# Two hand-overs between phases reshaped, and the second mixer's sigmoids and products in another order

## The chip, the core and the metric

One core of one Trainium2 chip. The metric is device time in microseconds of one execution; the kernel before has a median of 3087.38 us over three runs (3086.38 to 3090.63).

## The reference

One step of a small two-layer decoder for a prompt of 1024 tokens and a sample group of 8 sequences with 4 new tokens each, all in float32:

```python
h = x
for l in range(2):
    if l == 0:   # mLSTM matrix memory, 8 heads, chunks of 128 tokens; q,k,v,o and gate rows from one w_in
        mix = mlstm_layer(rmsnorm(h, norm_mix[0]), state_c, state_n, state_m, w_in_a, b_i, b_f, head_norm, w_out_a)
    else:        # one shared K/V from h, 16 heads of 64; the sample group also reads 1024 paged past keys
        k, v = split(rmsnorm(h, norm_kv) @ w_kv)
        q = rmsnorm(h, norm_mix[1]) @ w_q_b
        z = q @ k.T / 8 + sb_bias
        A[t, s] = sigmoid(z[t, s]) * prod(sigmoid(-z[t, j]) for s < j < t)      # stick-breaking, s < t
        mix = (A @ v) @ w_out_b
    h = h + mix
    h = h + square(relu(rmsnorm(h, norm_mlp[l]) @ w_up[l])) @ w_down[l]
y = rmsnorm(h, norm_final)
```

Outputs are y, the shared K/V rows and the mLSTM states, for the prompt and for the sample.

## The kernel before

**Data.** The 1024 + 32 tokens (T = 1056) lie along the free axis in NT = 3 tiles of TW = 352; the 1024 features are KT = 8 blocks of 128 partitions. The residual stream is `h`, 128 x 8 x 1056. A dense product of full precision is made from halves: ACT writes the rounded `xhi`, DVE writes `xlo` = x - xhi, GpSimd (POOL) does the same with every weight panel (128 output features, 512 KB; `split_panel`: an optional gain, a cast, a subtraction), and PE issues three matmuls per block. So a full tile of a panel is 24 matmuls of 352 columns (`dense_tile`), and one panel is three tiles. Raw panels and their halves have two buffers each; a panel may be loaded when the one two before it is split.

**Phases.** Each phase is a block in which every engine has its own written-out queue, with a barrier behind it: `constants` (masks, identity, gains), `embed` (x is turned by 36 groups of transposes into `h`), `mixer_a`, `out_and_mlp`, then semaphores are cleared, `mixer_b`, `out_and_mlp`, `final`. A phase's first two weight panels are loaded and split in the phase before (`head_loads`, `head_splits`). A norm is worked in the phase that needs it: `norm_act` gives the high halves of all blocks and their squares, `norm_dve` the low halves and the sum of the squares, `norm_pe` sums it over partitions, `norm_act_rs` makes the inverse root. PE meanwhile has `dense_first`, the first panel's three tiles together, block by block. In `mixer_a` the first panel (`last128`) holds the gate rows; they are stored to `graw` and regrouped by three products with `pick` (L830), which POOL's fills (L686 and on) must precede; the gate chain on DVE and the dense panels, in thirds of a tile (`third`), follow. `h` is put aside in memory (`spill`) so that its space can be used.

**The MLP.** `out_and_mlp` goes through the 4096 inner features in CH = 8 turns of a loop: per turn, four panels of w_up and four of w_down (two halves each); DVE adds each product tile to `h` at L2009, block by block, and PE uses banks 0, 1 and 2.

**The second mixer.** `mixer_b` works 8 pairs of heads, each in 8 slots. A slot is a tile of 128 queries of the prompt, from the longest (slot 0: 1024 keys, two chunks of 512 columns) to the shortest (slots 4 to 7 have one chunk of up to 512). PE computes the scores z into banks 3 and 4, one for each head of the pair (L1455). For each, ACT applies two sigmoids, of z and of -z (L1642, L1643); DVE multiplies up the second along the keys in a scan (L1785) and multiplies the two (L1791). PE turns the weights of the tile before (L1505, "pack" turns), ACT copies what is turned out of the banks (L1696), PE multiplies it with v (L1551). Between them lie turns of the sample's pages, and the next pair's q, k, v panels in thirds of tiles (`THIRDS_AT`); in the last pair there are none. The sample's weights for half of the sequences (`g`) are made at slots 0 and 4: ACT's sigmoids behind the last page turn of the slot before, DVE's scan and product over 1056 columns (`chain_sample`, L1797 and L1800), and PE's turn of them in the same slot ("sat", L1512), all by tables of slots:

```python
QUERIES_AT, SUMS_AT, SAT_AT, VALUES_AT, YS_AT = {-3: 0}, {0: 0, 4: 1}, {0: 0, 4: 1}, {1: 0, 5: 1}, {2: 0, 6: 1}
```

PE takes the turns of a slot in the order of `turns_of`: rows, pages mixed with packs, the sample's weights, its outputs. PE runs its queue in order, as each engine does.

## Time and profile before

| what | value |
| --- | --- |
| median of the runs | 3087.38 us (3086.38 to 3090.63) |
| profiled execution: time, span | 3094.23 us, 3092.4 us |
| mean granted TensorE clock | 0.974 |
| PE busy | 94% |
| DVE busy | 45% |
| ACT busy | 26% |
| POOL busy | 24% |

The profiled execution is one more execution of the same program, 0.2% above the median; rows are of it. In a timeline a row is start, duration, engine, line of kernel.py, operation, output and inputs, shapes, how many alike in a row (xN), and in brackets how long the engine had stood before it and what ended that. "PEq" or "SPq" is an engine's sequencer, "bank" an accumulation bank of PE.

### The profile page before, as it was taken

To read this page: it belongs to the slowest core of one execution; us is meant where nothing else is said; L and a number is where in the kernel's file an instruction comes from. 1 tells how busy PE (TensorE), PEld (TensorE's weight loads), DVE (VectorE), ACT (ScalarE), POOL (GpSimd) and SP (SyncE) were. 2 spreads that over 40 slices of the span, in tenths; PEclk is the share of its full clock that TensorE was granted. 3 is DMA by queue.
4 is the path that set the end of the run, shared out by engine and by line. 5 is a ranking of instruction groups with operands and counts; after the bars stand their busy time and mean duration, and the time that the engine had idled before them with its cause. 6 is when DMAs were issued, how large, how long until landed. Compare 5 with 4: busy or idle time off the path is not lost. (4 is left out here: it accounts for less than half of the span.)

```text
span 3092.4 us, 49344 instructions
## 1 busy us (share of the span) xinstructions
PE 2893.2 (94%) x19749; PEld 2634.2 (85%) x19749; DVE 1378.7 (45%) x1993; ACT 818.4 (26%) x1647; POOL 756.2 (24%) x452
## 2 busy tenths in 40 slices
PE   5999997999999999978999899898799999999998
PEld 4989887999999999976766677666599999999997
DVE  4422334444433344444546554655545433344434
ACT  3120222211110011124555545555512110011112
POOL 4212111322323323332111211120122332332331
PEclk8999998999999999989999999999899999999999
DMA  5666444233233232223333433343411111111112
GB/s 160 177 149 193 83 29 92 73 92 96 81 95 95 81 95 87 89 97 96 107 109 98 121 97 114 100 119 91 147 48 42 48 42 47 47 41 47 47 41 77
DMA packets 362482, 277.68 MB, mean 90 GB/s; under 512 B 31394, under 2 KB 353954, under 8 KB 360290
## 3 DMA queue, kind: packets, MB, share of 16 engines
q1 hardware_dynamic: 341002, 258.18, 28.8%
q10 hardware_dynamic: 21336, 17.47, 2.9%
q8 instruction: 104, 1.70, 0.2%
q14 instruction: 40, 0.33, 0.0%
HBM read 251.58 MB, written 91.11 MB: 111 GB/s over the span
## 5 line engine op out<-in xcount | busy, mean ns | idle before, releaser
L162 POOL CAST w_hi<-w_raw 128x1024 fp32r<-128x1024 f32 x194 | 208.6, 1075 | 1661.1 <-PE bank L214 902.0
L212 PE MATMUL bank<-p_u_hi,w_hi 128*128 128x352 f32 x1536 | 496.5, 323 | 14.5 <-DVE p_u_lo L2001 14.5
L212 PE MATMUL bank<-x_hi,w_hi 128*128 128x352 f32 x1536 | 496.9, 323 | 2.9 <-DVE p_q L1758 2.9
L213 PE MATMUL bank<-p_u_lo,w_hi 128*128 128x352 f32 x1536 | 495.5, 323 | 0.0
L214 PE MATMUL bank<-p_u_hi,w_lo 128*128 128x352 f32 x1536 | 495.3, 322 | 0.0
L214 PE MATMUL bank<-x_hi,w_lo 128*128 128x352 f32 x1536 | 494.5, 322 | 0.0
L213 PE MATMUL bank<-x_lo,w_hi 128*128 128x352 f32 x1536 | 494.0, 322 | 0.0
L164 POOL TENSOR_TENSOR w_lo<-w_raw,w_hi 128x1024 fp32r<-128x1024 f32 x194 | 483.8, 2494 | 15.6
L2009 DVE TENSOR_TENSOR h<-bank,h 128x352 f32<-128x352 f32 x384 | 199.9, 524 | 492.5 <-PE bank L214 492.5
L1961 ACT ACTIVATE p_relu<-bank 128x352 f32<-128x352 f32 x192 | 89.1, 464 | 1039.5 <-PE bank L214 1033.2
L212 PEld LDWEIGHTS bank<-p_u_hi,w_hi 128*128 128x128 f32 x1536 | 288.5, 188 | 18.7 <-issue 18.7
L212 PEld LDWEIGHTS bank<-x_hi,w_hi 128*128 128x128 f32 x1536 | 289.1, 188 | 4.7 <-issue 4.7
L213 PEld LDWEIGHTS bank<-x_lo,w_hi 128*128 128x128 f32 x1536 | 290.0, 189 | 0.0
L214 PEld LDWEIGHTS bank<-x_hi,w_lo 128*128 128x128 f32 x1536 | 289.3, 188 | 0.0
L214 PEld LDWEIGHTS bank<-p_u_hi,w_lo 128*128 128x128 f32 x1536 | 288.6, 188 | 0.0
L213 PEld LDWEIGHTS bank<-p_u_lo,w_hi 128*128 128x128 f32 x1536 | 288.6, 188 | 0.0
L1785 DVE TENSOR_TENSOR_SCAN square<-square,zero 128x512 f32<-128x512 f32 (+5 forms) x192 | 212.7, 1131 | 124.1 <-ACT square L1643 122.3
L1997 DVE TENSOR_TENSOR p_relu<-p_relu,rms_inverse 128x352 f32<-128x352 f32 x192 | 133.4, 695 | 275.5 <-ACT p_relu L1961 275.5
L1999 DVE CAST p_u_hi<-p_relu_sq 128x352 fp32r<-128x352 f32 x192 | 162.9, 849 | 108.5 <-ACT p_relu_sq L1963 108.5
L706 PE MATMUL bank<-x_hi,w_hi 128*128 128x352 f32 x576 | 200.0, 347 | 0.0
L708 PE MATMUL bank<-x_hi,w_lo 128*128 128x352 f32 x576 | 186.2, 323 | 0.0
L707 PE MATMUL bank<-x_lo,w_hi 128*128 128x352 f32 x576 | 185.8, 323 | 0.0
(247 smaller groups left out, 4587.7 us busy)
## 6 DMA issues: line engine op xcount, KB each, us to landing
k_pages<-in_cache_k SPq DMA_DIRECT2D x64, 512.0 KB, 5.7
w_raw<-in_w_up SPq DMA_DIRECT2D x64, 512.0 KB, 4.0
v_pages<-in_cache_v SPq DMA_DIRECT2D x64, 512.0 KB, 4.8
w_raw<-in_w_down SPq DMA_DIRECT2D x64, 512.0 KB, 3.4
p_pages<-k_pages SPq DMA_DIRECT2D x256, 128.0 KB, 2.4
p_pages<-v_pages SPq DMA_DIRECT2D x256, 128.0 KB, 2.3
w_raw<-in_w_in_a SPq DMA_DIRECT2D x26, 512.0 KB, 4.5
h<-h_spill ACTq DMA_DIRECT2D x16, 528.0 KB, 8.6
```

The costliest lines, as they stand in the source:

```text
L162: pool.tensor_copy(m.whi[slot][:, :], m.wraw[slot][:, :]).then_inc(w.hi, 1)
L164: pool.tensor_tensor(m.wlo[slot][:, :], m.wraw[slot][:, :], f32(m.whi[slot][:, :]), ALU.subtract)\
L212: pe.matmul(bank[:, 0:TW], wh, xh, start=(k == 0), stop=False)
L213: pe.matmul(bank[:, 0:TW], wh, xl, start=False, stop=False)
L214: last = pe.matmul(bank[:, 0:TW], wl, xh, start=False, stop=(k == nk - 1))
L706: pe.matmul(bank[:, 0:TW], wh, xh, start=(kk == 0), stop=False)
L707: pe.matmul(bank[:, 0:TW], wh, xl, start=False, stop=False)
L708: last = pe.matmul(bank[:, 0:TW], wl, xh, start=False, stop=(kk == KT - 1))
L1785: dve.tensor_tensor_scan(stick, stick, m.zero[:, 0:1].broadcast_to([P, hi - lo]), sticks[h2][:, hi:hi + 1] if x else 1.0, ALU.mult, ALU.ad ...
L1997: dve.tensor_tensor(relu[t][:, :], relu[t][:, :], m.rs[:, toks], ALU.mult).then_inc(scaled, 1)
L1999: dve.tensor_copy(uhi[:, u, toks], sqr[t][:, :]).then_inc(hi_ready, 1)
L2009: dve.tensor_tensor(ht, m.bank[t][:, 0:TW], ht, ALU.add).then_inc(w.tile_free[t], 1)
```

## The change

**The start.** `constants` and `embed` become one phase, `start`. x's loads are issued first; POOL makes the identity first, and the masks after; the gain of the first norm comes in a transfer of its own on ACT's queue. The first mixer's norm is done in it, in thirds of the tokens: transposes up to three, six and nine blocks of x (`TO`), copies out by ACT (two of three groups) and DVE (every third), the high and low halves of that third in pieces of 352 columns, squares of a third in one instruction into x's rows, and their sum by three halving additions. PE does the gate rows' tiles (`gates`) between the transposes, into banks 5 to 7, and the sums. POOL splits the first two panels within it, and SP stores the spill. In `mixer_a` the norm and `dense_first` are gone; PE does one tile of the first dense panel (`third(TAU0, ...)`) before the gate products, and the second copy of `last128`, which had no tiles, is no longer there.

```diff
+def start(nc, m, own):
+    AT_DVE = 3
+    TO = [3, 6, NB]
...
+        squares = [xin[:, a:a + 3, :].rearrange("p b d -> p (b d)")[:, 0:KT * TW] for a in (0, 3, 6)]
...
+        @block.sync
+        def _(sp):
+            for b in range(NB):
+                t0, n = blocks_of(b)
+                src = m.d["x_prompt"][0, t0:t0 + n, :] if b < NC else m.d["x_sample"].rearrange("b t d -> (b t) d")
+                sp.dma_start(xin[0:n, b, :], src).then_inc(landed[b], 16)
+                if b == TO[0] - 1:
+                    load_panel(sp, m, w, 0, m.heads[0].panels[0][0])
+            load_panel(sp, m, w, 1, m.heads[0].panels[1][0])
...
+            wait_taken(sp, 2 * NB)
+            for k in range(KT):
+                sp.dma_start(m.spill[k], m.h[:, k, :]).then_inc(m.heads[0].spilled, 16)
...
+            split(0)
...
+            split(1)
...
+            def gates(t):
+                pe.wait_ge(w.split, 1)
+                for k in range(KT):
+                    pe.wait_ge(s.x, t * KT + k + 1)
+                    wh, wl = m.whi[0][:, k * P:(k + 1) * P], m.wlo[0][:, k * P:(k + 1) * P]
+                    xh, xl = m.xhi[:, k, t * TW:(t + 1) * TW], m.xlo[:, k, t * TW:(t + 1) * TW]
+                    pe.matmul(m.bank[5 + t][:, 0:TW], wh, xh, start=(k == 0), stop=False)
+                    pe.matmul(m.bank[5 + t][:, 0:TW], wh, xl, start=False, stop=False)
+                    last = pe.matmul(m.bank[5 + t][:, 0:TW], wl, xh, start=False, stop=(k == KT - 1))
+                last.then_inc(w.tile_ready, 1)
+            def sums(t):
+                pe.wait_ge(s.acc, t + 1)
+                pe.matmul(m.bank[2 + t][:, 0:TW], m.ones[:, :], m.acc[:, t * TW:(t + 1) * TW], start=True, stop=True)\
+                    .then_inc(s.sum, 1)
+            for g in range(2 * TO[1]):
+                turn(g)
+            gates(0)
+            for g in range(2 * TO[1], 2 * NB):
+                turn(g)
+            gates(1)
+            pe.wait_ge(made, 2)
+            wait_taken(pe, 2 * NB)
+            sums(0)
+            gates(2)
+            sums(1)
+            sums(2)
...
+            def copies(t):
+                for g in range(2 * TO[t - 1] if t else 0, 2 * TO[t]):
+                    if g % AT_DVE:
+                        take(act, act.copy, free_act, g)
+            def high(t):
+                ts = slice(t * TW, (t + 1) * TW)
+                wait_taken(act, 2 * TO[t])
+                if t == 0:
+                    act.wait_ge(gain_in, 16)
+                for k in range(KT):
+                    act.activation(m.xhi[:, k, ts], m.h[:, k, ts], ACT.Copy, scale=m.g_mix[0][:, k:k + 1]).then_inc(s.hi, 1)
...
+            copies(0)
+            high(0)
+            copies(1)
+            high(1)
+            square(0)
+            copies(2)
+            high(2)
+            square(1)
+            square(2)
+            act.wait_ge(made, 2)
+            norm_act_rs(act, m, s, 2)
...
+            copies(0)
+            wait_taken(dve, 2 * TO[0])
+            dve.wait_ge(gain_in, 16)
+            low(0)
+            copies(1)
+            wait_taken(dve, 2 * TO[1])
+            low(1)
+            copies(2)
+            add(0)
+            wait_taken(dve, 2 * TO[2])
+            low(2)
+            add(1)
+            add(2)
...
@@ mixer_a: PE, ACT @@
-            dense_first(pe, m, w, 0, 0, 0, s.x)
-            norm_pe(pe, m, s)
+            for part in range(len(THIRDS)):
+                third(TAU0, part)
...
-            for tau in range(TAU0, TAU0 + FIRST_TILES):
+            for tau in range(TAU0 + 1, TAU0 + FIRST_TILES):
...
-            norm_act(act, m, s, m.h, m.g_mix[0])
-            for kk in range(KT):
-                act.dma_start(m.spill[kk], m.h[:, kk, :]).then_inc(spilled, 16)
-            norm_act_rs(act, m, s)
```

**The middle.** The last of the first MLP's eight turns is written out behind the loop. In it ACT takes the high half and the square of each block of `h` once its three additions are done, and DVE the low half and the squares' addition, between its additions. PE ends the phase with `dense_first` for w_q_b's first panel, into banks 5 to 7, with the norm's sums between its blocks six and seven; SP stores the spill there. `mixer_b` starts without a norm, its first three tiles are read out at once, and the biases' negatives are made behind the fifth tile.

```diff
@@ out_and_mlp: SP, PE, ACT, DVE @@
+                for k in range(KT):
+                    for t in range(NT):
+                        sp.wait_ge(w.tile_free[t], USES_OUT + (CH - 1) * USES_C + UT + k + 1)
+                    sp.dma_start(m.spill[k], m.h[:, k, :]).then_inc(after.spilled, 16)
...
-            with pe.Fori(1, CH) as i:
+            with pe.Fori(1, CH - norm_after) as i:
                 turn(i, 0)
+            if norm_after:
+                turn(CH - 1, 0)
+                def sums():
+                    pe.wait_ge(w.tile_free[2], USES_OUT + CH * USES_C)
+                    norm_pe(pe, m, after.s, 2)
+                dense_first(pe, m, after.w, 0, 0, 0, after.s.x, between=sums, at=KT - 2, bank0=5)
...
+                for k in range(KT):
+                    for t in range(NT):
+                        act.wait_ge(w.tile_free[t], USES_OUT + (CH - 1) * USES_C + UT + k + 1)
+                    act.activation(m.xhi[:, k, :], m.h[:, k, :], ACT.Copy).then_inc(after.s.hi, 1)
+                    norm_square(act, m, after.s, m.h, k)
+                norm_act_rs(act, m, after.s, 2)
...
+                    if ending:
+                        dve.wait_ge(after.s.hi, k + 1)
+                        dve.tensor_tensor(m.xlo[:, k, :], m.h[:, k, :], f32(m.xhi[:, k, :]), ALU.subtract).then_inc(after.s.x, 1)
+                        norm_add(dve, m, after.s, k)
```

**The second mixer.** ACT's sigmoids are given out by head instead of for both heads together: one head's two, then a copy of a turn, then the next head's. DVE's `chain_sample` stands behind the tile's first chunk (`chain_of(p, n, 0)`) instead of ahead of it. PE's queue has the same order as before.

```diff
@@ mixer_b: SP, PE, ACT, DVE @@
-            for kk in range(KT):
-                eng.dma_start(m.spill[kk], m.h[:, kk, :]).then_inc(spilled, 16)
...
-            dense_first(pe, m, w, 0, 0, 0, s.x)
-            norm_pe(pe, m, s)
...
-            norm_act(act, m, s, m.h, None)
-            norm_act_rs(act, m, s)
...
+            def gates(p, n, x, h2):
...
-                if tiles:
-                    gates(p, n, 0)
+                due = [(x, h2) for x in range(len(CHUNKS[n])) for h2 in range(2)] if tiles else []
+                if due:
+                    gates(p, n, *due.pop(0))
                 for i, y in enumerate(turns):
                     read_turn(y)
-                    if i == 1 and lower:
-                        gates(p, n, 1)
+                    if due and (due[0][0] == 0 or i):
+                        gates(p, n, *due.pop(0))
                     if i and turns[i - 1][0] == "page" and turns[i - 1][2][2] == SG - 1:
                         gates_sample(turns[i - 1][1], *turns[i - 1][2][:2])
+                if slot == EARLY:
+                    act.wait_ge(landed, 48)
+                    act.wait_ge(chain, 2)
                 if turns and turns[-1][0] == "page" and turns[-1][2][2] == SG - 1:
                     gates_sample(turns[-1][1], *turns[-1][2][:2])
-                if len(turns) < 2 and lower:
-                    gates(p, n, 1)
+                for x, h2 in due:
+                    gates(p, n, x, h2)
...
-            norm_dve(dve, m, s, m.h, None)
-            dve.wait_ge(landed, 48)
-            dve.wait_ge(filled, 1)
-            dve.tensor_scalar(nbias[:, :], bias[:, :], -1.0, None, ALU.mult).then_inc(chain, 1)
...
+                if tau == NT + 1:
+                    dve.wait_ge(landed, 48)
+                    dve.tensor_scalar(nbias[:, :], bias[:, :], -1.0, None, ALU.mult).then_inc(chain, 1)
...
-                for pc, g in at(SUMS_AT, slot):
-                    chain_sample(pc, g)
...
                     chain_of(p, n, 0)
+                for pc, g in at(SUMS_AT, slot):
+                    chain_sample(pc, g)
```

On DVE, around the barrier between the first MLP and the second mixer, there stood before (`h<-bank,h` is the MLP's addition, L284 the low halves, L292 and L295 the squares' sum, L1758 q's read-out):

```order
L2009 TENSOR_TENSOR h<-bank,h 128x352
L1992 REGISTER_ALU
L1992 COMPARE_AND_BRANCH
L1838 UNCONDITIONAL_BRANCH
L1742 UNCONDITIONAL_BRANCH
L284 SCALAR_TENSOR_TENSOR x_lo<-h,x_hi 128x1056 x8
L292 COPY squares<-square 128x1056
L295 TENSOR_TENSOR squares<-squares,square 128x1056 x7
L1747 TENSOR_SCALAR p_minus_bias<-p_bias 128x16
L1748 TENSOR_SCALAR p_minus_bias_sample<-p_bias_sample 128x8
L1758 SCALAR_TENSOR_TENSOR p_q<-bank,rms_inverse 128x352 x3
L1776 COPY p_q_sample<-p_q 64x8x4 x2
```

With the change the same place reads:

```order
L2126 TENSOR_TENSOR h<-bank,h 128x352 x3
L2129 TENSOR_TENSOR x_lo<-h,x_hi 128x1056
L295 TENSOR_TENSOR squares<-squares,square 128x1056
L1934 UNCONDITIONAL_BRANCH
L1838 UNCONDITIONAL_BRANCH
L1849 SCALAR_TENSOR_TENSOR p_q<-bank,rms_inverse 128x352 x3
L1867 COPY p_q_sample<-p_q 64x8x4 x2
L1855 TENSOR_TENSOR p_k<-bank,rms_inverse 128x352 x2
L1905 TENSOR_SCALAR p_minus_bias<-p_bias 128x16
L1906 TENSOR_SCALAR p_minus_bias_sample<-p_bias_sample 128x8
```

The low halves and the squares' additions have moved between the MLP's additions, and behind the barrier the read-outs of q and k come first.

On DVE in slot 4 of a pair (the first two rows are the end of slot 3, and the last row is slot 5's; L1797 and L1800 are the sample's scan and product, L1785 and L1791 the tile's) the order before was:

```order
L1785 SCALAR_TENSOR_TENSOR square<-square,zero 128x511 x2
L1791 TENSOR_TENSOR p_weights<-p_weights,square 128x512 x2
L1805 COPY h<-bank 128x128
L1797 SCALAR_TENSOR_TENSOR squares<-squares,zero 128x1056
L1800 TENSOR_TENSOR p_weights_sample<-p_weights_sample,squares 128x1055
L1785 SCALAR_TENSOR_TENSOR square<-square,zero 128x511 x2
L1791 TENSOR_TENSOR p_weights<-p_weights,square 128x511 x2
L1764 TENSOR_TENSOR p_k<-bank,rms_inverse 128x352
L1805 COPY h<-bank 128x128
```

And with the change:

```order
L1876 SCALAR_TENSOR_TENSOR square<-square,zero 128x511 x2
L1882 TENSOR_TENSOR p_weights<-p_weights,square 128x512 x2
L1896 COPY h<-bank 128x128
L1876 SCALAR_TENSOR_TENSOR square<-square,zero 128x511 x2
L1882 TENSOR_TENSOR p_weights<-p_weights,square 128x511 x2
L1888 SCALAR_TENSOR_TENSOR squares<-squares,zero 128x1056
L1891 TENSOR_TENSOR p_weights_sample<-p_weights_sample,squares 128x1055
L1855 TENSOR_TENSOR p_k<-bank,rms_inverse 128x352
L1896 COPY h<-bank 128x128
```

The sample's scan and product have moved behind the tile's two scans and two products.

On ACT in the same slot (L1655 and L1656 are the sample's sigmoids, L1642 and L1643 the tile's, L1696 and L1703 copies of turned weights), before:

```order
L1655 ACTIVATE p_weights_sample<-bank,p_bias_sample 128x512
L1656 ACTIVATE squares<-bank,p_minus_bias_sample 128x512
L1642 ACTIVATE p_weights<-bank,p_bias 128x512
L1643 ACTIVATE square<-bank,p_minus_bias 128x511
L1642 ACTIVATE p_weights<-bank,p_bias 128x512
L1643 ACTIVATE square<-bank,p_minus_bias 128x511
L1696 COPY p_weights_t<-bank 128x256
L1696 COPY p_weights_t<-bank 128x512 x2
L1703 COPY p_weights_sample_t<-bank 128x512 x2
```

And with the change:

```order
L1747 ACTIVATE p_weights_sample<-bank,p_bias_sample 128x512
L1748 ACTIVATE squares<-bank,p_minus_bias_sample 128x512
L1734 ACTIVATE p_weights<-bank,p_bias 128x512
L1735 ACTIVATE square<-bank,p_minus_bias 128x511
L1788 COPY p_weights_t<-bank 128x256
L1734 ACTIVATE p_weights<-bank,p_bias 128x512
L1735 ACTIVATE square<-bank,p_minus_bias 128x511
L1788 COPY p_weights_t<-bank 128x512 x2
L1795 COPY p_weights_sample_t<-bank 128x512 x2
```

The first pack copy now stands between the two heads' sigmoids.

## Rows read from the trace of the kernel before

**Rows 1.** The page: busy us of each engine, its share of the span, instructions.

```profile
PE 2893.2 (94%) x19749; PEld 2634.2 (85%) x19749; DVE 1378.7 (45%) x1993; ACT 818.4 (26%) x1647; POOL 756.2 (24%) x452
```

**Rows 2.** Waits of PE in the second mixer, 1415 to 2230: us, times, longest.

```profile
PE bank L1551 <- ACT p_weights_t L1696: 24.3, 29, 2.1
...
PE bank L1505 <- DVE p_weights L1791: 14.7, 8, 4.3
```

**Rows 3.** Timeline of PE before the first mixer's panels: start, us, row.

```profile
65.22 3.56 PE L830 MATMUL bank<-square,p_pick_gates 128*128 128x352 f32 x6 [3.47 <-DVE square L1046]
...
68.35 0.59 PE L706 MATMUL bank<-x_hi,w_hi 128*128 128x352 f32 x1
```

**Rows 4.** Timeline of other engines in the same stretch.

```profile
10.27 3.87 SPq L391 DMA_DIRECT2D p_x_rows<-in_x_prompt  x8
...
14.08 6.24 PE L410 MATMUL bank<-identity,p_x_rows 128*128 128x128 f32 x40 [14.08 <-DMA p_x_rows<-in_x_prompt]
...
33.04 8.65 ACT L261 ACTIVATE x_hi<-h,g_mix 128x1056 fp32r<-128x1056 f32 x8 [7.64 <-PEq L380]
...
40.59 1.58 POOL L686 COPY p_pair_rows<-identity 8x512 f32<-8x512 f32 x1
```

**Rows 5.** Timeline of four engines from the first MLP's end on.

```profile
1346.36 0.52 DVE L2009 TENSOR_TENSOR h<-bank,h 128x352 f32<-128x352 f32 x1 [1.40 <-PE bank L214]
...
1349.68 2.34 POOL L164 TENSOR_TENSOR w_lo<-w_raw,w_hi 128x1024 fp32r<-128x1024 f32 x1
...
1353.62 7.90 ACT L261 ACTIVATE x_hi<-h 128x1056 fp32r<-128x1056 f32 x8 [52.42 <-PEq L2085]
...
1354.74 9.44 DVE L284 SCALAR_TENSOR_TENSOR x_lo<-h,x_hi 128x1056 fp32r<-128x1056 f32 x8 [7.85 <-ACT x_hi L261]
...
1401.76 0.43 PE L212 MATMUL bank<-x_hi,w_hi 128*128 128x352 f32 x1
```

**Rows 6.** SP's timeline, and DMA issues of 1350 to 1405 (last: us to landing).

```profile
1355.50 0.62 SPq L1372 DMA_DIRECT2D w_raw<-in_w_kv  x1
...
w_raw<-in_w_kv SPq DMA_DIRECT2D x1, 512.0 KB, 13.3
```

**Rows 7.** Timeline of slot 4 of the second pair.

```profile
1577.63 2.36 DVE L1797 TENSOR_TENSOR_SCAN squares<-squares,zero 128x1056 f32<-128x1056 f32 x1 [2.02 <-ACT squares L1656]
...
1578.16 0.68 ACT L1643 ACTIVATE square<-bank,p_minus_bias 128x511 f32<-128x511 f32 x1
...
1580.02 1.26 DVE L1800 TENSOR_TENSOR p_weights_sample<-p_weights_sample,squares 128x1055 f32<-128x1055 f32 x1
...
1583.44 1.27 DVE L1791 TENSOR_TENSOR p_weights<-p_weights,square 128x511 f32<-128x511 f32 x2
...
1583.54 0.66 PE L1512 MATMUL bank<-identity,p_weights_sample 128*128 128x128 f32 x4
```

**Rows 8.** Timeline of slots 0 and 1 of the second pair.

```profile
1522.08 2.36 DVE L1797 TENSOR_TENSOR_SCAN squares<-squares,zero 128x1056 f32<-128x1056 f32 x1 [2.78 <-ACT squares L1656]
...
1524.43 1.90 POOL L158 TENSOR_TENSOR w_raw<-w_raw,g_kv 128x1024 f32<-128x1024 f32 x1 [24.70 <-DMA w_raw<-in_w_kv]
...
1524.47 2.97 DVE L1800 TENSOR_TENSOR p_weights_sample<-p_weights_sample,squares 128x1055 f32<-128x1055 f32 x1
...
1527.37 5.30 DVE L1785 TENSOR_TENSOR_SCAN square<-square,zero 128x512 f32<-128x512 f32 x2
...
1529.53 0.60 PE L1512 MATMUL bank<-identity,p_weights_sample 128*128 128x128 f32 x4
...
1532.58 1.26 DVE L1791 TENSOR_TENSOR p_weights<-p_weights,square 128x511 f32<-128x511 f32 x2
...
1539.39 1.13 PE L1455 MATMUL bank<-p_k,p_q 64*128 64x512 f32 x4 [1.20 <-ACT square L1643]
```

**Rows 9.** A stall of pair 0, and a window just behind: busy, then granted clock.

```profile
1436.25 1.33 PE L1455 MATMUL bank<-p_k,p_q 64*128 64x512 f32 x4 [2.88 <-ACT square L1643]
...
1438.00:1439.00 1.00, 1.00 (x16) 0.64 (x18) 0.63 (x3) 1.00 (x3) 0.00 (x0) 0.50 0.07 16
```

More of the change, by code:

```diff
@@ L111, in weight_turns @@
         per, per_tiles = len(panels), sum(x[1] for x in panels)
-        assert per % 2 == 0
+        assert per % 2 == 0 or (turns == 1 and panels is stages[-1][1])
         def turn(i, last, n0=n, t0=tiles, panels=panels, per=per, per_tiles=per_tiles):
@@ L189, in head_loads @@
         if w is not None:
-            sp.wait_ge(w.split, panels - 1 + slot)
+            sp.wait_ge(w.split, panels - (panels + slot + 1) % 2)
         load_panel(sp, m, head.w, slot, ap)
@@ L226, in dense_panel, with dense_first @@
         dense_tile(pe, m.whi[slot], m.wlo[slot], KT, 0, m.xhi, m.xlo, t, m.bank[t]).then_inc(w.tile_ready, 1)
-def dense_first(pe, m, w, n, slot, before, x, between=None):
+def dense_first(pe, m, w, n, slot, before, x, between=None, at=KT // 2, bank0=0):
     pe.wait_ge(w.split, n + 1)
@@ L236, in dense_first @@
     for k in range(KT):
-        if k == KT // 2 and between is not None:
+        if k == at and between is not None:
             between()
@@ L398, in _ @@
         @block.tensor
         def _(pe):
-            g = 0
-            for b in range(NB):
-                n = blocks_of(b)[1]
-                pe.wait_ge(landed[b], 16)
-                for half in range(2):
-                    if g >= 4:
-                        pe.wait_ge(free_act if g % 2 else free_dve, (g - 4) // 2 + 1)
-                    for q in range(4):
-                        k = 4 * half + q
-                        last = pe.transpose(m.bank[g % 4][:, q * P:q * P + n], xin[0:n, b, k * P:(k + 1) * P],
-                                            m.ident[0:n, 0:n])
-                    last.then_inc(turned, 1)
-                    g += 1
@@ L415, in read_out, with turn @@
-        def read_out(eng, op, which, free):
-            for g in range(which, 2 * NB, 2):
-                t0, n = blocks_of(g // 2)
-                eng.wait_ge(turned, g + 1)
-                src = m.bank[g % 4][:, :].rearrange("p (q t) -> p q t", q=4)[:, :, 0:n]
-                op(m.h[:, 4 * (g % 2):4 * (g % 2) + 4, t0:t0 + n], src).then_inc(free, 1)
+            def turn(g):
+                n = blocks_of(g // 2)[1]
+                if g == 0:
+                    pe.wait_ge(ident_made, 2)
+                pe.wait_ge(landed[g // 2], 16)
+                if g >= 4:
+                    pe.wait_ge(*((free_dve, taken_by_dve(g - 3)) if (g - 4) % AT_DVE == 0 else (free_act, g - 3 - taken_by_dve(g - 3))))
+                for q in range(4):
+                    k = 4 * (g % 2) + q
+                    last = pe.transpose(m.bank[g % 4][:, q * P:q * P + n], xin[0:n, g // 2, k * P:(k + 1) * P], m.ident[0:n, 0:n])
+                last.then_inc(turned, 1)
@@ L422, in _, with copies, low @@
         @block.vector
         def _(dve):
-            read_out(dve, dve.tensor_copy, 0, free_dve)
-        @block.scalar
-        def _(act):
-            read_out(act, act.copy, 1, free_act)
+            def copies(t):
+                for g in range(2 * TO[t - 1] if t else 0, 2 * TO[t]):
+                    if g % AT_DVE == 0:
+                        take(dve, dve.tensor_copy, free_dve, g)
+            def low(t):
+                ts = slice(t * TW, (t + 1) * TW)
+                for k in range(KT):
+                    dve.wait_ge(s.hi, t * KT + k + 1)
+                    dve.scalar_tensor_tensor(out=m.xlo[:, k, ts], in0=m.h[:, k, ts], scalar=m.g_mix[0][:, k:k + 1],
+                                             in1=f32(m.xhi[:, k, ts]), op0=ALU.mult, op1=ALU.subtract).then_inc(s.x, 1)
@@ L1011, in _ @@
         def _(dve):
-            norm_dve(dve, m, s, m.h, m.g_mix[0])
             step = Pipe(dve, chain)
@@ L1832, in _, with out_and_mlp @@
                         sample_queries(pq)
-def out_and_mlp(nc, m, own, w_out, w_up, w_down, gain, gather, head, after):
+def out_and_mlp(nc, m, own, w_out, w_up, w_down, gain, gather, head, after, norm_after):
     with ExitStack() as c:
@@ L1955, in _, with turn @@
             m.outputs = []
-            with act.Fori(0, CH) as i:
+            def turn(i):
                 for u in range(UT):
@@ L1963, in _ @@
                         act.activation(sqr[t][:, :], relu[t][:, :], ACT.Square).then_inc(sq_ready, 1)
+            with act.Fori(0, CH - norm_after) as i:
+                turn(i)
+            if norm_after:
+                turn(CH - 1)
+                for k in range(KT):
+                    for t in range(NT):
[3 more added lines that the diff above has]
+                norm_act_rs(act, m, after.s, 2)
         @block.vector
@@ L1991, in _, with turn @@
             dve.wait_ge(s.rs, 1)
-            with dve.Fori(0, CH) as i:
+            def turn(i, ending):
                 for u in range(UT):
@@ L2076, in program @@
         m.outputs = []
-        phase(constants)
-        phase(embed)
+        phase(start)
         phase(mixer_a)
-        phase(out_and_mlp, d["w_out_a"][0], d["w_up"][0], d["w_down"][0], m.g_mlp[0], True, m.heads[1], m.heads[2])
+        phase(out_and_mlp, d["w_out_a"][0], d["w_up"][0], d["w_down"][0], m.g_mlp[0], True, m.heads[1], m.heads[2], 1)
         done.extend(owners[0].sems + owners[1].sems)
```

178 lines of the change are left out of this document (98 added, 80 removed).

## The prediction

> **What bounds the kernel now.** I began with the page: PE is busy for 94% of the span [rows 1], so only time in which PE stands can be won, and whatever makes PE stand is paid in full. The waits of PE and its timeline show three places that this change touches. At the start PE's first real panel tile begins at 68.35 us [rows 3]: before it lie a phase for constants, a phase that turns x, and the whole norm. Behind the first MLP PE ends its last tile at 1346.3 (DVE's last addition starts at 1346.36) and begins the second mixer's third panel at 1401.76 [rows 5]: 55.5 us for two panels (six tiles) and a few turns of pages, some 27 us of work. In the second mixer PE's stalls are short and many: for ACT's copies 24.3 us in 29 waits, for DVE's products 14.7 in 8 [rows 2].
>
> A full tile of 24 matmuls costs PE 3.8 us: DVE's addition waits 1.40 us and takes 0.52, so a half tile of 12 comes each 1.92 us, 0.16 us a matmul [rows 5].
>
> **The start.** The phase of constants goes; x's loads, issued at 10.27, come at about 2.3 (an estimate, a little behind the 1.6 us of a phase's beginning, below), and the first transpose, 3.8 us after the issue before (14.08) [rows 4], at about 6.1, or 7 with the gain's small transfer beside it. Norm work is cut in thirds between the transposes. ACT then has the high halves (8.65 us before [rows 4], more in 24 smaller pieces: estimate 11), 12 copies of x (7), the squares (7.5): 26 us. DVE has 6 copies, 24 low halves and 9 additions: about 25 us, and some 5 behind POOL, whose two splits now fall there. They wait for one another, and the sums come last. I put the phase's end at 43.5, between 40 (ACT never waits) and 46.
> Then the first mixer's own work. PE computes one panel tile at once (4 to 6 us), but the gate rows need POOL's fills. Before, they took from 33.04 to 42.17, 9.1 us [rows 4], and lay under the norm; now nothing else covers them. With DVE quiet they may take 6.5. The gate products after them took 3.1 us until 68.35 at the slow clock [rows 3], 1.9 if not. Together 8.4 to 12.2 after the phase's start; I take 9.1, as DVE is quiet. PE is through them at 52.6 instead of 68.35: **-15.8 us**. The tile done ahead is no further gain: only two banks serve the panel tiles, and DVE reads them between the steps of the gate chain, which starts no sooner than the gates; PE waits for banks instead.
>
> **The middle.** The norm moves into the MLP's last turn. After the last tile PE has six of eight parts of the first query tile (54 matmuls, 8.6 us), the sums (1.9) and the rest (2.9): 13.4 us, to 1359.7. From POOL's end at 1352.0 to the next phase's first instruction at 1353.62 is 1.6 us [rows 5], so the phase begins at 1361.3, 7.7 later than before. There the spill and the norm are gone. PE's next three tiles start at once (11.5 us), but now the transfers are late: the panel after them (w_kv, issued at 1355.5, 1.9 us after the phase's start) took 13.3 us to land [rows 6], behind the biases' tiny pieces. 15.2 us after the start it is in, perhaps 14 without the spill behind it; POOL's gain, cast and difference (1.90 [rows 8], 1.04, 2.34 [rows 5]) make 5.4 more. So the third panel begins 20.5 us after the phase's start; before, at 1401.76 [rows 5], 48.1 after. Gain: 48.1 - 20.5 - 7.7 = 19.9.
> Against it stands DVE in the last turn. Per 5.76 us (three tiles) it now has three additions (1.5), a low half of 1.18 (9.44 / 8 [rows 5]) and a squares' addition of about 1.4, after ACT's high half of 1.07: 4.8 us from the first to PE's next need, so one of slack. But at every second block POOL begins its split at just that moment. DVE's product of 1055 columns takes 1.26 alone [rows 7] and 2.97 when POOL's multiply began 0.04 before it, which took its usual 1.90 [rows 8]. So two such operations lose some 2.2 us, less the slack 1.1, at three blocks: 3.4 us. The Trainium skill (SBUF — State Buffer, "Who interferes with whom") says that a VectorE instruction with two SBUF inputs and a GpSimd one that reads SBUF lock each other out for the whole instruction; the trace agrees (2.97 against 1.26). By that rule the turn loses about these 3.4 us, by DVE's uncontended rows alone nothing. The sum takes 3.4, bounds 0 and 7: **-16.5 us**.
>
> **The second mixer: products behind the first chunk.** PE turns the sample's weights (L1512) in the same slot in which DVE makes them, and this order stays. In slot 4 DVE starts the sample's scan at 1577.63, ends its product at 1581.3, then does the tile's two scans and two products until 1584.7; PE comes at 1583.54 and needn't wait [rows 7]. In the new order DVE starts when the first head's second sigmoid ends, 1578.84, stands 0.25 us for the second head (a copy is between), and has the same 7.1 us of work, the sample's last: it ends at 1586.4. PE stands there for 2.9 us. In slot 0 POOL is in the way too. DVE's same work runs without a gap from 1522.08 to 1533.84 [rows 8], 11.8 us of which 4.6 are POOL's. In the new order it starts at 1523.3, stands 0.5, and ends at 1535.7, while PE comes at 1529.53: 6.2 us. That replaces PE's waits for the tile's own products (1.7) and for the next z (1.20), and the next chunk is later; followed on to the z that began at 1539.39 [rows 8], PE is 3.5 us later. Pair 0 gives 4, pair 7 (no panels to fill with) 2.4 and 4.6. Over eight pairs: slot 0 27, slot 4 25: **+52 us**.
>
> **Sigmoids by head.** A copy is now 1.2 us earlier where it stood behind both heads. In slot 3 the longest of ACT's copy waits, 2.0 us in each pair (the longest of all is 2.1 [rows 2]), falls to 0.8: -1.2 × 8. In slot 2 a page copy that PE waits for comes earlier, but the next copy doesn't, since ACT is full there; PE stands at the next step: 0. The small ones and pair 7's add 3. Together **-12.6 us**, at best -25 (half of all ACT waits in [rows 2]). Moved sigmoids delay DVE's second scan by up to 0.7, hidden under five us of PE's work, except in slots 0 and 4, counted above.
>
> **The clock.** After PE had stood 2.88 us until 1436.25, its granted clock was 0.50, the 1.2 GHz level [rows 9], for about 3.5 us, which costs 1.7. Before, such stretches come once to three times a pair. The new stalls make one in slot 0 and probably one in slot 4, and spare that of slot 3. I take +2 in all, bounds -10 and +15.
>
> **Sum:** -15.8 - 16.5 + 52 - 12.6 + 2 = +9 us on the profiled execution's 3094.2. The median of the runs is 0.2% lower, 3087.4; the same 9 us on it make **3096.5 us**.
>
> **Rivals.**
> *The hand-overs win.* Slot 4's and slot 0's products come in time, because PE reaches the sample's turn later than I think or makes the loss good at its next waits. For it: DVE's work is the same in both orders, and before PE waits for DVE all the same (14.7). Against: PE's place in slot 4 is fixed by its own full work, and behind it stand no DVE waits to take the loss. With a quarter of the 52 left: 3096.5 - 39 = 3057.5. It decides once slot 4 costs less than 1 us and slot 0 less than 2.
> *Half of it.* The two stalls are there, but ACT's earlier copies return 25 instead of 12.6 (3084), and the phase at the start ends at 40 (3080.5) or the slow clock spares 10: down to 3074.
> *Worse.* Each new stall brings the slow clock (+15), and the last turn loses 7 or the panel of the middle comes later: 3112 to 3120. For it: the clock row; against: the slow stretches that are there already.
> *The hand-overs don't do what they say*: the start's phase is bound by ACT and DVE, which wait for one another at each third, and ends at 50, the fills come on top. For it: both engines have over 25 us of work in it; against: they had it before too, one after the other. It costs 6.5 us more: 3103.
>
> **Chances.** Forecast (3088 to 3108) 0.45; half of it 0.2; hand-overs win 0.17; worse and hand-overs weak 0.18. About 0.2%, 6 us, is what the measurement can tell from no change. Faster by more than that is the winning rival and half of the second, 0.27; within it is the other half and the low end of the forecast, 0.2; slower 0.53. The range leaves out most of the winning rival and the worst end: 3066 to 3114.
>
> **What would show it.** PE at the sample's first turn (L1512 before) waiting for DVE's sample product: sixteen waits, 2.9 us in slot 4 and about 6 in slot 0; if these are under 1 and 2, the largest term is wrong. PE's gate products ending near 52.6, and waits of the tile after them for a bank. The second mixer's third panel about 20 us after its phase's start, released by POOL behind w_kv; three stalls of about 1.1 us in the last turn, just after POOL begins a split. The copy wait of 2.0 in slot 3 gone to 0.8. Wrong would be the whole if DVE's sample scan were found ahead of its need in slot 4, or if the phase at the start ended past 48.

## The result, and the profile after

The changed kernel has a median of 3123.49 us over four runs (3119.78 to 3125.12), beside 3088.77 us for the kernel before: a ratio of 1.0111 with an interval of 1.0094 to 1.0129, so 34.7 us slower (29 to 40). The forecast was 9 us slower, 3096.5, with a range that ended at 3114. The side was right and the size was not.

The page of the profiled execution (3119.78 us), engine by engine, answers to [rows 1]; PE is busy for 93% now:

```profile
PE 2898.8 (93%) x19749; PEld 2632.8 (84%) x19749; DVE 1385.8 (44%) x2007; ACT 822.6 (26%) x1661; POOL 745.4 (24%) x450
```

**The start** went nearly as forecast. PE's timeline (start, us, engine, line, operation) at the gate products, for [rows 3], and at the beginning of `mixer_a`:

```profile
46.88 0.63 PE L812 MATMUL bank<-x_hi,w_hi 128*128 128x352 f32 x1 [2.01 <-PEq L328]
...
53.56 1.94 PE L935 MATMUL bank<-square,p_pick_gates 128*128 128x352 f32 x6
...
55.07 0.59 PE L812 MATMUL bank<-x_hi,w_hi 128*128 128x352 f32 x1
...
60.63 0.40 PE L812 MATMUL bank<-x_hi,w_hi 128*128 128x352 f32 x1 [1.29 <-DVE p_v_next L1138]
```

In the new phase PE's last sums ended at 44.9 and ACT's inverse roots at 46.6 (forecast for the phase's end: 43.5), and PE's first product of `mixer_a` came at 46.88. The gate products were done at 55.1 (forecast 52.6) where they were done at 68.35 before: 13.3 us won, not 15.8. And the tile computed ahead was followed by a wait for a bank, as forecast.

**The middle** too. In the last turn PE stood twice for 0.7 us for DVE's addition (forecast: three times 1.1). Just before each of the two, DVE's low half took 3.0 us beside POOL's subtraction, where it takes 1.26 alone. Behind the barrier the third panel began at 1369.11, 22.6 us after the phase's first instruction (forecast 20.5, before 48.1 by [rows 5]), because w_kv again took 13.2 us to land [rows 6] and the pages were as late:

```profile
1301.24 0.43 PE L212 MATMUL bank<-p_u_hi,w_hi 128*128 128x352 f32 x1 [0.70 <-DVE h L2126]
1313.75 0.43 PE L212 MATMUL bank<-p_u_hi,w_hi 128*128 128x352 f32 x1 [0.71 <-DVE h L2126]
...
1363.81 3.63 PE L1585 MATMUL bank<-identity,p_pages 128*128 128x128 f32 x16 [5.59 <-DMA p_pages<-k_pages]
...
1369.11 0.43 PE L212 MATMUL bank<-x_hi,w_hi 128*128 128x352 f32 x1
```

**The second mixer** is where the time went. The waits of PE from its first z to its last (what PE waited for: us, times, longest), for [rows 2]:

```profile
PE bank L1611 <- DVE p_weights_sample L1891: 72.3, 16, 7.8
PE bank L1664 <- DMA p_pages<-v_pages: 21.5, 20, 2.6
PE bank L1650 <- ACT p_weights_t L1788: 20.9, 36, 1.0
PE bank L1635 <- ACT p_page_keys_t L1776: 8.7, 14, 0.7
PE bank L1585 <- ACT p_page_keys_t L1776: 5.6, 16, 0.4
PE bank L1554 <- ACT square L1735: 4.5, 3, 2.1
```

The sixteen waits for the sample's product are there. In pairs 1 to 6 they have the two sizes foretold, 5.7 to 6.05 us in slot 0 and 2.81 in slot 4; pair 0 has 7.8 and 2.81, and the last pair 4.5 and 5.0. PE's timeline in slots 0 and 4 of the second pair, for [rows 8] and [rows 7]:

```profile
1511.87 1.09 PE L1611 MATMUL bank<-identity,p_weights_sample 128*128 128x128 f32 x4 [6.04 <-DVE p_weights_sample L1891]
...
1565.75 1.09 PE L1611 MATMUL bank<-identity,p_weights_sample 128*128 128x128 f32 x4 [2.81 <-DVE p_weights_sample L1891]
```

But the four transposes behind the wait take 1.08 to 1.09 us at thirteen of the sixteen places, where they took 0.60 and 0.66 in the rows of before [rows 7, 8]. Windows of one us behind the first of these waits (length, busy us of PE, PEld, DVE, ACT, POOL; then the granted clock):

```profile
1513.00:1514.00 1.00, 1.00 (x6) 0.67 (x7) 1.00 (x2) 0.58 (x1) 0.00 (x0) 0.50 0.00 0
1515.00:1516.00 1.00, 1.00 (x4) 0.28 (x4) 0.91 (x3) 0.41 (x2) 0.00 (x0) 0.50 0.00 0
1517.00:1518.00 1.00, 1.00 (x8) 1.00 (x7) 0.12 (x1) 1.00 (x3) 0.00 (x0) 0.86 0.00 0
1518.00:1519.00 1.00, 1.00 (x10) 0.79 (x13) 0.84 (x1) 1.00 (x3) 0.00 (x0) 1.00 0.00 0
```

The clock is at its 1.2 GHz level until a little past 1517, five us into full work. By the granted clock in the trace such a stretch lies at fifteen of the sixteen waits (none at slot 4 of pair 6). The stretch from the first z to the last, first of the kernel before and then of the changed one, shows both parts of the loss (length, PE's busy us and instructions first):

```profile
1418.00:2212.50 794.50, 709.06 (x6047) 524.00 (x6043) 437.06 (x548) 424.93 (x894) 121.45 (x62) 0.97 0.38 108
```

```profile
1385.40:2241.00 855.60, 721.58 (x6045) 529.74 (x6043) 448.03 (x548) 425.81 (x894) 118.00 (x64) 0.94 0.35 100
```

The first z comes 32.6 us earlier (forecast 32.3), and the stretch is 61.1 us longer: PE stands 134.0 us for 85.4, and is busy 12.5 us more with the same instructions. The profiles' times differ by 25.6 us only, the runs by 34.7, since the profiled execution of the changed kernel is the fastest of its four and that of before lies 5.5 us above its median. It had a mean granted clock of 0.974, while the other runs of before, taken beside the experiments, had 0.975 to 0.980. So the busy time read from it is above the usual: three other kernels below that keep the old order in the mixer have 3 to 8 us less.

### The profile page after: what moved, and what is told of

It reads as the page before. It is cut to its first block and busy times, and to the rows that moved or that the text cites. A ratio compares the mean times of both kernels' runs of the same rounds, so it can differ in the third digit from the quotient of the medians.

```text
span 3117.9 us, 49333 instructions
## 1 busy us (share of the span) xinstructions
PE 2898.8 (93%) x19749; PEld 2632.8 (84%) x19749; DVE 1385.8 (44%) x2007; ACT 822.6 (26%) x1661; POOL 745.4 (24%) x450
## 5 line engine op out<-in xcount | busy, mean ns | idle before, releaser
L164 POOL TENSOR_TENSOR w_lo<-w_raw,w_hi 128x1024 fp32r<-128x1024 f32 x193 | 478.1, 2477 | 15.5
```

Source lines behind the costliest of these rows:

```text
L164: pool.tensor_tensor(m.wlo[slot][:, :], m.wraw[slot][:, :], f32(m.whi[slot][:, :]), ALU.subtract)\
```

## The experiments

They ran in three sets of four, each set on one chip, with the kernel before beside it: its medians there were 3086.92, 3087.81 and 3087.55 us. A ratio is to the kernel before in the same set. The changed kernel was timed apart from them (3088.77 beside it), so a difference to its 3123.5 is uncertain by a further us or two. Four ways to split the change came first.

**The sample's work ahead again**, all else as changed:

```diff
                 if p < PAIRS:
                     chain_of(p, n, 0)
-                for pc, g in at(SUMS_AT, slot):
-                    chain_sample(pc, g)
```

(and the two lines put back ahead of the `if`.)

> The changed kernel, with DVE's sample scan and product ahead of the tile's first chunk again; all else as changed. Theory (the order of DVE is the loss): the sixteen waits for the sample's product, 72.3 us in the changed kernel's profile, go; about 19 us of other waits come back, and some 10 us of slow clock behind the stalls goes too. 3123.5 - 63 = about 3060 (3054 to 3068), with PE busy in the second mixer back from 722 us to about 710. Rival (DVE's total work is the bound, whatever its order): the waits move to the tile's own products and the next z, and at most 20 us come back: 3103 or more.

Measured: 3053.93 us (3053.41 to 3054.85), ratio 0.9888 (0.9868 to 0.9907). It is 69.6 us faster than the changed kernel and beats the kernel before by 33. Its stretch between the first and last z:

```profile
1389.00:2176.30 787.30, 697.76 (x6047) 513.07 (x6043) 446.80 (x548) 424.96 (x894) 126.67 (x64) 0.98 0.38 109
```

Against the changed kernel PE stands 44.5 us less (89.5) and is busy 23.8 us less. Time and busy part (expected near 710) fell a little further than the theory said. DVE's total work is the same, so the rival falls.

**The two hand-overs alone.** `chain_sample` ahead and `gates(p, n, x)` for both heads, as before (a part of the edit):

```diff
-                due = [(x, h2) for x in range(len(CHUNKS[n])) for h2 in range(2)] if tiles else []
-                if due:
-                    gates(p, n, *due.pop(0))
+                if tiles:
+                    gates(p, n, 0)
...
```

> The changed kernel with both edits of the second mixer's order taken back (sample ahead, sigmoids for both heads together), so the two hand-overs alone. Theory: the hand-overs are worth the 32 us by which the first z came earlier in the profile, 3088.8 - 32 = 3056, and the by-head sigmoids next to nothing, so this lies 2 to 6 us above the run with only the sample's work ahead (3060 to 3066 by that). Rival by the prediction (by-head sigmoids are worth 12.6): 12 to 13 us above that run, some 3073. Rival (the hand-overs' gain in the profile isn't whole in the runs, whose difference was 34.7 where the profiles' was 25.6): 3066.

Measured: 3062.56 us (3058.6 to 3066.9), ratio 0.9921 (0.9899 to 0.9942): 24 us faster than before (18 to 31), and 8.6 slower than the run above, between the theory's 2 to 6 and the rival's 12 to 13.

**The second mixer's edits alone**, on the kernel before (both hunks of `mixer_b` on ACT's loop and DVE's order, no hand-over).

> The kernel before with the second mixer's two edits alone (sample behind the first chunk, sigmoids by head), no hand-over changed. Theory: the mixer's stretch took 61 us longer in the profile (48.5 of standing, 12 of slow clock), and does so here: 3088.8 + 61 = 3150 (3144 to 3160). Rival (the loss needs the changed hand-overs, which shift PE's start against the pages): well below 3140.

Measured: 3148.0 us (3146.12 to 3150.16), ratio 1.0192 (1.0171 to 1.0213), 61 us slower. The loss needs no hand-over.

**The sigmoids by head alone**, on the kernel before.

> The kernel before with the sigmoids by head alone. Prediction: -12.6 us, 3076. Theory from the two profiles (copies' waits 23.1 to 20.9, page turns' 11.6 to 5.6, pages of v by DMA 17.1 to 21.5): -4, 3085, with the longest copy wait down from 2.1 to 1.0 but more small ones. Rival (the second head's sigmoid is late for DVE and PE's z): 3092 or more.

Measured: 3080.32 us (3073.41 to 3082.03), ratio 0.9975 (0.9965 to 0.9985): 6.6 us faster, between the theory's 4 and the prediction's 12.6. The same stretch in this kernel, and in the one with both edits:

```profile
1420.30:2200.60 780.30, 695.56 (x6045) 512.02 (x6043) 444.72 (x548) 424.74 (x894) 123.58 (x64) 0.99 0.38 110
```

```profile
1418.10:2269.20 851.10, 724.13 (x6046) 530.57 (x6043) 445.92 (x549) 425.34 (x894) 123.11 (x64) 0.94 0.35 101
```

Between these two only the sample's place differs. It costs 67.7 us in the medians, and 70.8 in the profiles, of which 42.2 us are standing (84.7 to 127.0) and 28.6 us PE's busy time. And beside the kernel before, the sigmoids by head saved no standing (85.4 to 84.7). The longest wait for a copy did fall:

```profile
PE bank L1551 <- ACT p_weights_t L1695: 22.3, 39, 1.0
PE bank L1565 <- DMA p_pages<-v_pages: 19.8, 17, 2.6
```

There are 39 waits for 29 [rows 2], though. PE waits 6 us less for the turned pages of keys, but more for z (15.5 us for 11.1), for DVE's products (15.5 for 14.7) and for the pages of v (19.8 for 17.1).

**The new stalls filled with useless work.** This asks whether the low clock comes from the standing.

```diff
                     if part == 0:
+                        for i in range((18 if g else 40)):
+                            pe.transpose(bank[:, 0:P], q[p % 2][:, 0:P], m.ident[:, :])
                         pe.wait_ge(as_ready, p * 2 + g + 1)
```

> The changed kernel, with PE given useless transposes (40 in slot 0, 18 in slot 4, into the bank that the sample's turn then overwrites) ahead of its sixteen waits for the sample's product. They add work and save no wait: they only keep PE from standing for the 2.8 and 6 us. Theory (standing brings the low clock behind it; profiles: 18 low stretches in the changed kernel, 5 with the sigmoids by head alone): the stretches behind these waits go, 20 to 28 us: 3096 to 3104, with a mean clock of 0.98 or more. Rival (the low clock comes from something else in these slots, such as all engines working together): no stretch goes, 3123 to 3130, a little slower by fillers that end late.

Measured: 3100.04 us (3098.18 to 3101.32), ratio 1.0037 (1.0025 to 1.005). With 464 more instructions on the engine that bounds the kernel it is 23.5 us faster than the changed kernel, at a mean clock of 0.984 to 0.986 for 0.971 to 0.973. A hundred us of the second pair, in the changed kernel, with the fillers, and with the sample's work ahead:

```profile
1500.00:1600.00 100.00, 86.06 (x731) 64.12 (x730) 57.16 (x69) 49.52 (x106) 16.83 (x9) 0.95 0.34 97
```

```profile
1500.00:1600.00 100.00, 91.97 (x804) 70.35 (x801) 55.44 (x68) 48.94 (x105) 15.87 (x9) 0.98 0.33 96
```

```profile
1500.00:1600.00 100.00, 91.03 (x792) 67.95 (x791) 57.94 (x72) 53.95 (x114) 18.38 (x10) 1.00 0.39 112
```

From the first z to the last, all of PE and then the useless transposes alone:

```profile
1386.10:2220.40 834.30, 753.31 (x6509) 567.03 (x6507) 448.27 (x548) 425.20 (x894) 117.64 (x62) 0.98 0.36 103
```

```profile
1386.10:2220.40 834.30, 56.54 (x464) 53.71 (x464) 0.98 0.36 103
```

PE's own work took 753.3 - 56.5 = 696.8 us there, 24.8 less than in the changed kernel. The fillers took 56.5 us and PE stood 81.0 beside them, 3.5 together above the 134.0 of standing; they did not close the waits wholly (17.0 us are left in 15 of them). So the clock's part of the loss is shown: some 25 us of PE's own work, of which 23.5 came back in the time.

**Slot 0 ahead, slot 4 behind.**

```diff
                 for pc, g in at(SUMS_AT, slot):
-                    chain_sample(pc, g)
+                    if g == 1:
+                        chain_sample(pc, g)
```

(g == 0 ahead of `chain_of`.)

> The changed kernel, with the sample's products ahead of the first chunk in slot 0 only, behind it in slot 4. Theory (2.81 us of standing in slot 4 in each pair, and a low stretch of some 1.4 us behind it): 8 x 4.2 = 34 us above the run with both ahead, 3053.9 + 34 = 3088. By the prediction's price for slot 4 (25 us, no clock): 3079. Rival (slot 4's wait is mostly made good later in the pair): 3065 or less, all of the loss being slot 0's.

Measured: 3084.21 us (3082.06 to 3093.39), ratio 0.9995 (0.9983 to 1.0007). Slot 4 costs 30 us (3084.2 - 3053.9) and slot 0 39 us (3123.5 - 3084.2). The 30 lie between the theory's 34 and the prediction's 25. Its eight waits, all in slot 4:

```profile
PE bank L1611 <- DVE p_weights_sample L1891: 24.7, 8, 5.0
```

**The start's hand-over alone**: the new phase and first mixer, with `out_and_mlp` and `mixer_b` of the kernel before.

> The kernel before with the hand-over at the start alone. Prediction -15.8: 3071. Theory from the profile (gate products end at 55.1 for 68.6, -13.5): 3073 to 3074. Rival (the gate chain or the panels' loads make it late again before the first MLP): 3080 or more.

Measured: 3072.93 us (3071.5 to 3074.2), ratio 0.9949 (0.9931 to 0.9967), 14.9 us faster.

**The middle's hand-over alone**: the new last turn and the second mixer without a norm, in its old order.

> The kernel before with the hand-over between the first MLP and the second mixer alone, the second mixer's order as before. Prediction -16.5: 3070. Theory from the profiles (first z 32.6 earlier, 13.5 of it the start's): -19, 3068. Rival (part of it is given back in the second mixer, whose pages and panels are now late against PE): -10 or less, 3077.

Measured: 3070.17 us (3064.98 to 3073.94), ratio 0.9936 (0.9917 to 0.9956), 17.6 us faster.

**The kernel before with its own longest copy wait filled.** If the sigmoids by head won only clock, fillers would win it too.

```diff
+                    if x == 0 and (p or n):
+                        pe.wait_ge(y_ok, p * SLOTS + n)
+                    if n == 2 and x == 0:
+                        for i in range(12):
+                            pe.transpose(m.bank[7][:, 0:P], q[p % 2][:, 0:P], m.ident[:, :])
                     pe.wait_ge(turn_read, TURN_NO[y] + 1)
-                    if x == 0 and (p or n):
-                        pe.wait_ge(y_ok, p * SLOTS + n)
```

The wait for `y_ok` moves ahead with them, since the transposes write into bank 7, which it guards.

> The kernel before, with twelve useless transposes on PE in slot 3 of each pair, ahead of its longest wait for ACT's copy (1.97 us), nothing else. Theory (the sigmoids by head won no standing time, PE's idle in the mixer was 85.4 us before and 84.7 with them, but 13.5 us of busy time, because the long copy wait brings the low clock behind it): this wins the same by adding work, the low stretches fall from 15 to about 7, 6 to 13 us faster, 3075 to 3081 on a median of 3087. Rival (the by-head gain is from waits and the order, the clock by chance): no gain, 3087 to 3090.

Measured: 3090.79 us (3084.82 to 3093.74), ratio 1.0009 (1.0000 to 1.0018): no time was won, as the rival said. The wait was filled all but 0.66 us:

```profile
1465.27 1.47 PE L1548 MATMUL bank<-identity,p_q 128*128 128x128 f32 x12
1467.40 0.66 PE L1554 MATMUL bank<-p_weights_t,p_v_rows 128*64 128x128 f32 x8 [0.66 <-ACT p_weights_t L1699]
```

The time alone doesn't decide what it was to decide, though. From the first z to the last, all of PE and the useless transposes alone:

```profile
1417.70:2208.90 791.20, 710.16 (x6141) 526.25 (x6139) 438.56 (x548) 424.91 (x894) 124.86 (x63) 0.98 0.38 108
```

```profile
1417.70:2208.90 791.20, 11.79 (x96) 10.73 (x96) 0.98 0.38 108
```

PE's own work took 710.2 - 11.8 = 698.4 us, and it stood 81.0. The other profiles, in the same stretch (PE's own work, its standing, and by the granted clock the time at 1.2 GHz and the number of such stretches):

| kernel | sigmoids | own work | standing | at 1.2 GHz |
| --- | --- | --- | --- | --- |
| before | both heads | 709.1 | 85.4 | 54.6 in 14 |
| hand-overs alone | both heads | 705.8 | 86.7 | 47.8 in 13 |
| start alone | both heads | 703.4 | 87.8 | 41.0 in 11 |
| middle alone | both heads | 701.6 | 88.2 | 37.5 in 10 |
| before, wait filled | both heads | 698.4 | 81.0 | 34.1 in 7 |
| sigmoids by head alone | by head | 695.6 | 84.7 | 20.5 in 4 |
| sample's work ahead | by head | 697.8 | 89.5 | 23.9 in 5 |
| the same again | by head | 698.6 | 85.5 | 27.3 in 5 |
| loads first | by head | 698.9 | 83.9 | 27.3 in 6 |
| DVE's products by head too | by head | 707.1 | 82.0 | 47.8 in 9 |
| changed | by head | 721.6 | 134.0 | 99.0 in 17 |

So the fillers did shorten PE's own work, to what it takes with the sigmoids by head. But their 11.8 us of work took the place of only 4 to 7 us of standing, and that used the gain up. The sigmoids by head (the first four rows of them, with the sample's work ahead) change the standing by nothing clear and have 3 to 14 us less own work than the first four kernels: what they win seems to lie at the low clock. This rests on one profile of each kernel, one of them (DVE's products by head too, the run below) doesn't fit, and no run isolates it.

**Two tries at more**, on the kernel with the sample's work ahead. First, SP's order at the second mixer's start; the loads of the biases stood ahead of all of it (a part of the edit):

```diff
-            for n in range(2, 4):
-                weights(n)
+            weights(2)
             for l in range(PB):
                 load_page(l)
                 loads += 1
+            with nc.allow_non_contiguous_dma(reason="a row's bias, 8 KB"):
+                eng.dma_start(bias[:, :], m.d["sb_bias"][0:1, :].broadcast_to([P, HB])).then_inc(landed, 16)
...
+            weights(3)
```

> The best so far (changed kernel, sample's work ahead), with SP's queue at the second mixer's start in another order: the w_kv panel, eight pages, then the biases' tiny pieces, then w_q_b. Theory (the tiny pieces, 10 us to land, hold w_kv's 13.3 us and the pages; PE stands 5.6 us for the pages and starts the third panel 23 us after the phase's first instruction): both come 5 to 8 us earlier, 3054 - 6 = 3048. Rival (the biases now come too late and DVE, which waits for them before it reads the sixth tile, holds PE instead; or the pages are slowed by w_kv): 3052 to 3060.

Measured: 3045.39 us (3043.9 to 3051.81), ratio 0.987 (0.9854 to 0.9886). The panel now lands in 5.2 us, and PE no longer stands for the pages:

```profile
w_raw<-in_w_kv SPq DMA_DIRECT2D x1, 512.0 KB, 5.2
w_raw<-in_w_q_b SPq DMA_DIRECT2D x1, 512.0 KB, 12.6
```

Then DVE's product of a head right behind its scan, besides:

```diff
-                top = c1 if x else c1 - 1
-                for h2 in range(2):
+                    top = c1 if x else c1 - 1
                     dve.wait_ge(scanned, u + h2 + 1)
```

> The same as the run with the loads first, and DVE's product of a head right behind its own scan, instead of two scans and then two products. Theory (with the sigmoids by head DVE stands about 0.4 us between the two scans, which the product can fill; PE waits 15.3 us for these products): 2 to 5 us less, 3044 to 3046. Rival (the product waits for its scan's end, which costs more in each of 96 chains): 3048 to 3053.

Measured: 3048.75 us (3041.58 to 3051.86), ratio 0.9866 (0.985 to 0.9882). It can't be told from the run before it; its waits for DVE's products are 18.2 us for 16.3, so the two to five us of the theory are not seen.

The base for both, the sample's work ahead once more, in the same set:

> The changed kernel with the sample's work ahead once more, as the base beside which the two runs before it are read on this chip: 3054, within 3 us.

Measured: 3052.6 us (3050.08 to 3057.91), ratio 0.9892 (0.9877 to 0.9908). The loads' order is worth 7 us beside it (its first z is at 1386.6, with the loads first at 1379.9), though the two intervals overlap a little. The version with the loads first, 42 us below the kernel before, is the fastest of the study.

## Why the prediction was wrong

**The start (-15.8): right.** 14.9 us faster alone. The phase ended three us later than said (its end took in ACT's inverse roots, at 46.6, just past the upper bound of 46), and the gate products were done 8.2 us after the next phase's first instruction (46.84) instead of 9.1. The fills took 6.3 us (forecast 6.5) and were a near second: POOL was through at 53.1, and PE's extra tile, at the low clock until about 52.9, ended at 53.56.

**The middle (-16.5): right**, 17.6 us alone, and by the path foretold: the panel behind w_kv and the biases' tiny pieces. The contention of DVE and POOL in the last turn cost 1.4 us instead of 3.4. Together the two gave 24 us (18 to 31) for a forecast 32.3; the sum of the two alone, 32.5, lies just above that, and the scatter of the three runs covers the difference.

**Products behind the first chunk (+52, and the clock's +2): the side right, the size not.** The waits were sized right in pairs 1 to 6: 2.81 us for 2.9 (the terms as written, 1578.84, 0.25 and 7.1, end at 1586.2 and give 2.7) and 5.7 to 6.05 for 6.2. PE made good 23 to 30 us of them at its other waits, where 21 were reckoned: 72.3 us of waits became 42 to 49 net for 52. The whole edit cost 68 to 70 us.

**The step that failed is "The clock. [...] I take +2 in all, bounds -10 and +15."** Its own price, 1.7 us behind a wait of 2.88, makes 27 us for sixteen new waits. It counted one stretch in slot 0 and "probably" one in slot 4, and set against them the one of slot 3 in each pair, which left next to nothing. The runs show a low stretch at fifteen of the sixteen waits. In slot 0 it is 6.8 us long in seven pairs (1510.5 to 1517.3 in the second) and 10.2 in the last; in slot 4 it is 3.4 us in five pairs (1565.1 to 1568.5 in the second) and 6.8 in two. By itself the edit costs 23 to 29 us of PE's busy time; with the stalls filled, 23.5 us came back. The stretches that the sigmoids by head spare did vanish, but they gave back much less: PE's busy time in the changed kernel, 721.6, is still 12.5 to 20 us above that of the four profiles with the old order. That is what the +2 was to be, and three of the four differences lie above its upper bound of 15. The third rival ("each new stall brings the slow clock") had the mechanism and was given too small a price.

**Sigmoids by head (-12.6): half, and by another path.** 6.6 us measured alone, 8.6 behind the hand-overs. The 2.0 us wait of slot 3 did fall, to 0.82, but PE's standing did not: the time came back as more, shorter waits and at the pages of v. So the step "falls to 0.8: -1.2 × 8" priced a wait as if nothing stood behind it. What was won is, by the table above, most likely time at the low clock (six of the fourteen low stretches of before lay behind that wait), which the prediction had booked under the clock; this is read from profiles and not isolated by a run.

**The sum** by the runs alone: -14.9 - 17.6 + 67.7 - 6.6 = +28.6, just under the measured +29 to +40; with the hand-overs' joint 24.4 it is +36.7. Of the 25.7 us that the forecast of +9 missed, the clock behind the new waits makes more than twenty and the sigmoids six, against three to ten in which the standing was overestimated; the scatter of the sum takes the rest.

## What to carry to other kernels

Where the bounding engine is made to stand again and again, price the standing and then the low clock behind each new wait in full, and take off only those stretches whose own wait is shown to vanish; useless work put ahead of the wait tells the two apart in one run, if the engine's own work is read from the profile and not the time alone, since the useless work has a price too. Work whose consumer sits in the same slot of another engine's fixed queue must not go behind work whose consumer comes a slot later, however idle its own engine is (DVE was busy 44%, and the order cost 68 to 70 us). And one profile is one sample of the clock: compare its mean clock with that of the other runs before busy times of two profiles are subtracted.

## What was not expected of the hardware

- Around a wait of about 6 us PE's granted clock was at the 1.2 GHz level for 6.8 us (1510.5 to 1517.3), of which the last five were full work; at five of seven waits of 2.8 us for 3.4. PE's four transposes took 1.09 us in such a stretch and 0.60 to 0.66 outside.
- In the kernel before, six of the eight waits of 1.97 us were followed by such a stretch of 3.4 us (1467.8 to 1471.2 behind the first).
- 464 useless transposes on PE made the changed kernel 23.5 us faster.
- A 512 KB panel issued behind three loads of tiny pieces landed in 13.2 us, and ahead of them in 5.2.
